# Down phase of a decoder step: second weight parts added by accumulating transfers, weight differences on VectorE, h loads given out earlier

## The chip, the cores and the metric

The kernel is one program on one core of a Trainium2 chip. It is judged by its time on the device in microseconds, the median of several runs. Five queues matter here: TensorE (PE), VectorE (DVE), ScalarE (ACT), GpSimd (POOL) and SyncE (SP). Each works its own instructions strictly in order and meets the others through semaphores only.

## What is computed

One step of a two-layer decoder: an mLSTM layer, then a layer of sliding-window attention, each followed by an MLP with squared ReLU, over 1024 prompt tokens and 32 sample tokens (1056 columns), width 1024, inner width 4096, all in float32.

```python
def sq_relu_mlp(x, w_up, w_down):
    h = jax.nn.relu(x @ w_up)
    return (h * h) @ w_down

# in trunk, after each layer's mixer
x = x + sq_relu_mlp(rmsnorm(x, norm_ffn[l]), w_up[l], w_down[l])
```

The change touches only the second product of each MLP, `(h * h) @ w_down`, which is done once in each layer.

## The kernel before

**Tiling.** Activations lie transposed: a feature per partition, 1056 tokens along the row. Every float32 operand is cut into a high and a low half (fp32r), and every product is three matmuls, high x high, low x high, high x low. ScalarE makes the high half (a copy), VectorE the low half (operand minus high half).

**The up phase** computes h in 16 blocks f = 0 to 15 of 256 inner features. Block f's rows z are scaled by VectorE (`scaled`) and stored to HBM as `h_rows` by SP (`store_h`), two rows of 528 KB a block. z lies in `z_even` for even f, in `act_a` and `act_b` for odd f.

**The down phase** takes blocks 0 to 13 by a scheme of seven products (Strassen's kind, table `DOWN`): w_down is quartered into parts (mh, kh) and h into parts (kh, nh); each product multiplies one part, or the sum or difference of two, of each. A product has KG = 7 groups, so q = 0 to 48 counts the groups; blocks 14 and 15 are left as a tail (q = 49 to 52) whose rows are computed plainly (`last_rows`, `last_down`). For a product i = q // 7:

| product | weight parts | h parts |
|---|---|---|
| 0 | (1,0) + (1,1) | (0,0) |
| 1 | (1,1) | (1,0) - (0,0) |
| 2 | (1,0) - (0,0) | (0,0) + (0,1) |
| 3 | (0,0) | (0,1) - (1,1) |
| 4 | (0,0) + (1,1) | (0,0) + (1,1) |
| 5 | (0,0) + (0,1) | (1,1) |
| 6 | (0,1) - (1,1) | (1,0) + (1,1) |

**A group q** goes like this. SP gives out `load_w(q)`: the first weight part into `down_raw(q)`, one of three buffers (`w_raw`, `w_raw_odd`, `w_third`, by q % 3), and, where the table has a second part, that one into `down_other(n)`, one of two buffers. Pool's `down_sum` (L1500) adds or subtracts the two in place (semaphore dw_sum). ScalarE's `w_high` (L1068) and VectorE's `w_low` (L1670) make w_hi and w_lo, two buffers each by q % 2. On the other side SP's `load_h` brings rows of h: parts (0,0), (0,1) and (1,1) once each, into b11, b12 and b22, which stay; part (1,0), in products 1 and 6, anew for each group into b21_even and b21_odd in turn. VectorE's `t_sum_of_h` (L1698) adds or subtracts two parts into t_sum_of, ScalarE (L1085) and VectorE (`t_low_of`, L1678) make t_hi and t_lo, in a ring of three. TensorE (`down`, L2762 to L2764) then does 48 matmuls of 264 columns. After each product ScalarE stages PSUM into act_a and act_b (`stage`, L1098), and VectorE adds that to x_res (`add_staged`, L1705) during the next product.

**The order.** It is written out by hand. `down_step(q)` on VectorE is w_low(q), t_low_of(q + 1), perhaps add_staged, t_sum_of_h(q + 2), perhaps h_low. On SP the loop is `load_h(q + 1)`, `load_w(q)`. The waits that matter: load_w(q) from q = 3 waits for w_low(q - 3); a load into b21 waits for the t_sum that read the same buffer two groups before; w_high(q) waits until TensorE is done with group q - 2. At the start of the phase SP has

```python
load_h(0)
load_h(1)
load_h(2)
load_w(1)
load_h(3)
load_w(2)
store_h(NF - 1)
```

The functions that the change touches, with the line numbers of the profile:

## Time and profile before

| what | us |
|---|---|
| median of three runs | 2336.6 (2334.8 to 2339.12) |
| the profiled execution's own time | 2334.56 |
| its span | 2332.7 |
| TensorE busy | 2251.5 (97%) |
| VectorE busy | 1566.6 (67%) |
| ScalarE busy | 1072.2 (46%) |
| Pool busy | 498.0 (21%) |
| down phase of layer 0 | about 898 to 1201 |
| down phase of layer 1 | about 1959 to 2262 |

TensorE is busy nearly all the time, so the kernel's time is TensorE's work plus the places where TensorE waits. In a timeline row the first number is the start, the second the time taken, and the bracket at the end is how long the engine had been idle before and what ended it. Rows of one kind that follow each other are merged, with their count.

### The profile page before, as it was taken

The numbers are of one execution on the slowest core, as the hardware profiler recorded it, in microseconds if no ns is written. First come the engines' busy times: TensorE is split into PE (matmuls) and PEld (weight loads), VectorE is DVE, ScalarE is ACT, GpSimd is POOL, SyncE is SP. The second block draws the span as 40 slices with busy tenths as digits, with TensorE's granted clock in tenths as the row PEclk, the third lists the DMA queues.
The fourth block names the chain that finished last, engine by engine and source line by source line (L and its number), as shares of the span: only waits on it lengthen the run. The fifth ranks groups of instructions, "written<-read, shape, count | busy, mean of one in ns | idle before, by whom it ended". The sixth has DMA issues, their size and how long they took to land. (4 is left out here: it accounts for less than half of the span.)

```text
span 2332.7 us, 41472 instructions
## 1 busy us (share of the span) xinstructions
PE 2251.5 (97%) x16886; PEld 2149.1 (92%) x16886; DVE 1566.6 (67%) x2516; ACT 1072.2 (46%) x2058; POOL 498.0 (21%) x403
## 2 busy tenths in 40 slices
PE   8999999999999999999989999999999999999989
PEld 7989898888999999999989877869999999999988
DVE  6555555569765566888966666565855666798873
ACT  4233222245766664433423454254666664343435
POOL 1000000013222223114312011013122223123323
PEclk9999999999999999999999999999999999999999
DMA  4111121102233336656631312101233336665541
GB/s 130 37 51 57 51 70 40 43 23 65 93 100 103 111 111 238 231 190 204 206 127 48 100 28 53 37 10 46 92 103 101 111 105 217 225 224 182 201 154 75
DMA packets 220928, 256.28 MB, mean 110 GB/s; under 512 B 27687, under 2 KB 144340, under 8 KB 220708
## 3 DMA queue, kind: packets, MB, share of 16 engines
q1 hardware_dynamic: 220596, 253.61, 33.4%
q8 instruction: 135, 2.21, 0.4%
q14 instruction: 53, 0.43, 0.1%
q10 hardware_dynamic: 144, 0.02, 0.0%
HBM read 211.84 MB, written 46.93 MB: 111 GB/s over the span
## 5 line engine op out<-in xcount | busy, mean ns | idle before, releaser
L2762 PE MATMUL acc<-t_hi,w_hi 128*128 128x264 f32 x1568 | 448.5, 286 | 23.0 <-DVE w_lo L1670 23.0
L2764 PE MATMUL acc<-t_hi,w_lo 128*128 128x264 f32 x1568 | 448.7, 286 | 0.0
L2763 PE MATMUL acc<-t_lo,w_hi 128*128 128x264 f32 x1568 | 448.7, 286 | 0.0
L2762 PEld LDWEIGHTS acc<-t_hi,w_hi 128*128 128x128 f32 x1568 | 297.8, 190 | 26.4 <-DVE w_lo L1670 26.4
L2764 PEld LDWEIGHTS acc<-t_hi,w_lo 128*128 128x128 f32 x1568 | 296.5, 189 | 0.0
L2763 PEld LDWEIGHTS acc<-t_lo,w_hi 128*128 128x128 f32 x1568 | 296.4, 189 | 0.0
L2728 PE MATMUL acc<-x_lo,w_hi 128*128 128x264 f32 x896 | 254.6, 284 | 0.0
L2729 PE MATMUL acc<-x_hi,w_lo 128*128 128x264 f32 x896 | 254.5, 284 | 0.0
L2727 PE MATMUL acc<-x_hi,w_hi 128*128 128x264 f32 x896 | 254.4, 284 | 0.0
L2483 PE MATMUL acc<-x_hi,w_hi 128*128 128x352 f32 x576 | 193.1, 335 | 1.4 <-DVE pair L1955 1.4
L2727 PE MATMUL acc<-T_hi,w_hi 128*128 128x264 f32 x672 | 190.9, 284 | 0.2
L2728 PE MATMUL acc<-T_lo,w_hi 128*128 128x264 f32 x672 | 190.7, 284 | 0.0
L2729 PE MATMUL acc<-T_hi,w_lo 128*128 128x264 f32 x672 | 190.3, 283 | 0.0
L2485 PE MATMUL acc<-x_hi,w_lo 128*128 128x352 f32 x576 | 185.8, 323 | 0.0
L2484 PE MATMUL acc<-x_lo,w_hi 128*128 128x352 f32 x576 | 185.4, 322 | 0.0
L2727 PEld LDWEIGHTS acc<-x_hi,w_hi 128*128 128x128 f32 x896 | 168.8, 188 | 0.0
L2728 PEld LDWEIGHTS acc<-x_lo,w_hi 128*128 128x128 f32 x896 | 168.7, 188 | 0.0
L2729 PEld LDWEIGHTS acc<-x_hi,w_lo 128*128 128x128 f32 x896 | 168.4, 188 | 0.0
L1678 DVE TENSOR_TENSOR t_lo<-t_sum_of,t_hi 128x1056 fp32r<-128x1056 f32 x70 | 132.3, 1890 | 1.8
L2727 PEld LDWEIGHTS acc<-T_hi,w_hi 128*128 128x128 f32 x672 | 126.6, 188 | 0.7 <-DVE w_lo L1643 0.7
L2728 PEld LDWEIGHTS acc<-T_lo,w_hi 128*128 128x128 f32 x672 | 126.6, 188 | 0.0
L2729 PEld LDWEIGHTS acc<-T_hi,w_lo 128*128 128x128 f32 x672 | 126.1, 188 | 0.0
(396 smaller groups left out, 5705.2 us busy)
## 6 DMA issues: line engine op xcount, KB each, us to landing
w_raw<-in_w_down SPq DMA_DIRECT2D x72, 512.0 KB, 5.0
w_raw_odd<-in_w_down SPq DMA_DIRECT2D x70, 512.0 KB, 4.9
b<-h_rows SPq DMA_DIRECT2D x42, 528.0 KB, 6.3
w_third<-in_w_down SPq DMA_DIRECT2D x34, 512.0 KB, 4.5
h_rows<-z_even SPq DMA_DIRECT2D x32, 528.0 KB, 2.7
w_raw<-in_w_up SPq DMA_DIRECT2D x32, 512.0 KB, 4.6
w_raw_odd<-in_w_up SPq DMA_DIRECT2D x32, 512.0 KB, 5.2
w_raw<-in_w_mlstm_in SPq DMA_DIRECT2D x24, 512.0 KB
```

Of the source, the lines that this page charges most:

```text
L1678: V.tensor_tensor(lo[:], src, hi[:].bitcast(F32), ALU.subtract).then_inc(dt_lo, 1)
L2483: T.matmul(block_of(g), hi, mh[:, span(b)], start=(kk == 0), stop=False)
L2484: T.matmul(block_of(g), hi, ml[:, span(b)], start=False, stop=False)
L2485: x = T.matmul(block_of(g), lo, mh[:, span(b)], start=False, stop=(kk == n_k - 1))
L2727: T.matmul(out[:, q], hi[:, k], mh[:, k, v], start=(k == 0), stop=False)
L2728: T.matmul(out[:, q], hi[:, k], ml[:, k, v], start=False, stop=False)
L2729: x = T.matmul(out[:, q], lo[:, k], mh[:, k, v], start=False, stop=(k == 3))
L2762: T.matmul(out[:, h], hi[:, c, rows], mh[:, c, v], start=(g == 0 and c == 0), stop=False)
L2763: T.matmul(out[:, h], hi[:, c, rows], ml[:, c, v], start=False, stop=False)
L2764: x = T.matmul(out[:, h], lo[:, c, rows], mh[:, c, v], start=False, stop=(g == KG - 1 and c == 1))
```

## The change

On SP, the order at the start of the down phase and the number of semaphores for the resident h loads are altered: all seven loads of product 0 are given out first, each waits for the landing of the one two before it (it was four), and the store of the last block's rows moves behind load_w(4). For products with a sum (0, 4, 5) SP no longer loads the second weight part. Pool issues a transfer from HBM that adds the second part onto the first in SBUF (`add_part`); it waits for the first part's landing and for the transfer two before it. For products with a difference (2, 6) SP loads both parts as before, and VectorE subtracts (`down_sum`), in step q for group q + 2, ahead of t_sum_of_h. ScalarE's w_high waits for whichever it is. At the end of the phase VectorE's w_low for the last three tail weights moves between the additions of the first rows.

```diff
-W_SUMS = [q for q in range(NG) if DOWN[q // KG][1] is not None]
+W_SUMS = [q for q in range(NG) if DOWN[q // KG][1] == SUB]
+W_ADDS = [q for q in range(NG) if DOWN[q // KG][1] == ADD]
...
-                    if op is not None:
+                    if op == SUB:
...
-                            if n >= 4:
-                                sp.wait_ge(db_loaded[n % 4], 16 * (turns(layer, n, len(RESIDENT), 4) - 1))
+                            if n >= 2:
+                                sp.wait_ge(db_loaded[n % 2], 16 * (turns(layer, n, len(RESIDENT), 2) - 1))
...
-                load_h(0)
-                load_h(1)
-                load_h(2)
+                for q in range(KG):
+                    load_h(q)
                 load_w(1)
-                load_h(3)
                 load_w(2)
-                store_h(NF - 1)
                 for q in range(3, NW):
-                    if q + 1 < NG:
+                    if KG <= q + 1 < NG:
                         load_h(q + 1)
                     load_w(q)
+                    if q == 4:
+                        store_h(NF - 1)
...
+                elif q in W_ADDS:
+                    n = W_ADDS.index(q)
+                    act.wait_ge(dw_added[n % 2], 16 * turns(layer, n, len(W_ADDS), 2))
...
-            def down_sum(layer, q):
-
-                n = W_SUMS.index(q)
+            def add_part(layer, q):
+
+                n, (mh, kh) = W_ADDS.index(q), DOWN[q // KG][2]
+                f = KG * kh + q % KG
+                part = io["w_down"][layer][2 * P * f:2 * P * f + 2 * P, 512 * mh:512 * mh + 512].rearrange("(k p) m -> p k m", p=P)
                 pool.wait_ge(dw_loaded[q % 3], 16 * turns(layer, q, NW, 3))
-                pool.wait_ge(dv_loaded[n % 2], 16 * turns(layer, n, len(W_SUMS), 2))
-                nc.gpsimd.tensor_tensor(down_raw(q), down_raw(q), down_other(n), DOWN[q // KG][1]).then_inc(dw_sum, 1)
+                if n >= 2:
+                    pool.wait_ge(dw_added[n % 2], 16 * (turns(layer, n, len(W_ADDS), 2) - 1))
+                pool.dma_start(down_raw(q).rearrange("p (k m) -> p k m", k=2), part, accum_op=ADD).then_inc(dw_added[n % 2], 16)
...
+            def down_sum(layer, q):
+
+                n = W_SUMS.index(q)
+                dve.wait_ge(dw_loaded[q % 3], 16 * turns(layer, q, NW, 3))
+                dve.wait_ge(dv_loaded[n % 2], 16 * turns(layer, n, len(W_SUMS), 2))
+                V.tensor_tensor(down_raw(q), down_raw(q), down_other(n), DOWN[q // KG][1]).then_inc(dw_sum, 1)
...
+                if q + 2 in W_SUMS:
+                    down_sum(layer, q + 2)
                 if q + 2 in T_SUMS:
                     t_sum_of_h(layer, q + 2)
...
+                    if n < 2 * TAIL - 1:
+                        down_step(0, NG + 1 + n)
...
                     last_row(0, k)
+                    if 0 < k < 2 * TAIL:
+                        down_step(1, NG + k)
...
-                for q in range(2, NW):
+                for q in range(2, NG + 1):
                     down_step(layer, q)
```

How the instructions stand, at the places that the prediction speaks of. First SP at the start of the down phase of layer 0, before the change, from the last block's neighbour to load_w(3) (b11 is the resident part (0,0) of h):

```order
L797 DMA h_rows0<-z_even 128x1056 [waits zz_ready] x2
L839 DMA b11<-h_rows0 128x2x528 [waits h_stored0,up_done]
L839 DMA b11<-h_rows0 128x2x528 [waits h_stored1,up_done]
L839 DMA b11<-h_rows0 128x2x528 [waits h_stored0,up_done]
L818 DMA w_raw_odd<-in_w_down 128x2x512 [waits op_lo]
L824 DMA w_raw_odd<-in_w_down 128x2x512
L839 DMA b11<-h_rows0 128x2x528 [waits h_stored1,up_done]
L818 DMA w_third<-in_w_down 128x2x512 [waits h_stored0]
L824 DMA w_raw<-in_w_down 128x2x512 [waits dw_sum]
L797 DMA h_rows0<-act_b 128x1056 [waits zz_ready]
L797 DMA h_rows0<-act_a 128x1056 [waits zz_ready]
L839 DMA b11<-h_rows0 128x2x528 [waits db_loaded0,h_stored0,up_done]
```

The same place with the change, from the third load of h on:

```order
L841 DMA b11<-h_rows0 128x2x528 [waits db_loaded0,h_stored0,up_done]
L841 DMA b11<-h_rows0 128x2x528 [waits db_loaded1,h_stored1,up_done]
L841 DMA b11<-h_rows0 128x2x528 [waits db_loaded0,h_stored0,up_done]
L841 DMA b11<-h_rows0 128x2x528 [waits db_loaded1,h_stored1,up_done]
L841 DMA b11<-h_rows0 128x2x528 [waits db_loaded0,h_stored0,up_done]
L820 DMA w_raw_odd<-in_w_down 128x2x512 [waits op_lo]
L820 DMA w_third<-in_w_down 128x2x512 [waits h_stored0]
L820 DMA w_raw<-in_w_down 128x2x512 [waits dw_lo]
L820 DMA w_raw_odd<-in_w_down 128x2x512 [waits dw_lo]
L799 DMA h_rows0<-act_b 128x1056 [waits zz_ready]
L799 DMA h_rows0<-act_a 128x1056 [waits zz_ready]
```

The four loads of h that stood behind load_w(1) are now ahead of it, five of them with a wait for an earlier one's landing, and the stores went behind load_w(4).

VectorE in product 6 of layer 0, steps 43 and 44, before:

```order
L1670 TENSOR_TENSOR w_lo<-w_raw_odd,w_hi 128x1024 [waits dw_hi]
L1678 TENSOR_TENSOR t_lo1<-t_sum_of,t_hi1 128x1056 [waits dt_hi]
L1705 TENSOR_TENSOR x_res<-x_res,act_a 128x2x528 [waits staged_rows]
L1698 TENSOR_TENSOR t_sum_of<-b21_even,b22 128x1056 [waits db_loaded1,ds_loaded0,dt_lo]
L1670 TENSOR_TENSOR w_lo<-w_third,w_hi 128x1024 [waits dw_hi]
L1678 TENSOR_TENSOR t_lo2<-t_sum_of,t_hi2 128x1056 [waits dt_hi]
L1705 TENSOR_TENSOR x_res<-x_res,act_b 128x2x528 [waits staged_rows]
L1698 TENSOR_TENSOR t_sum_of<-b21_odd,b22 128x1056 [waits db_loaded2,ds_loaded1,dt_lo]
```

The same steps with the change:

```order
L1684 TENSOR_TENSOR w_lo<-w_raw_odd,w_hi 128x1024 [waits dw_hi]
L1692 TENSOR_TENSOR t_lo1<-t_sum_of,t_hi1 128x1056 [waits dt_hi]
L1719 TENSOR_TENSOR x_res<-x_res,act_a 128x2x528 [waits staged_rows]
L1678 TENSOR_TENSOR w_raw<-w_raw 128x1024 [waits dv_loaded0,dw_loaded0]
L1712 TENSOR_TENSOR t_sum_of<-b21_even,b22 128x1056 [waits db_loaded1,ds_loaded0,dt_lo]
L1684 TENSOR_TENSOR w_lo<-w_third,w_hi 128x1024 [waits dw_hi]
L1692 TENSOR_TENSOR t_lo2<-t_sum_of,t_hi2 128x1056 [waits dt_hi]
L1719 TENSOR_TENSOR x_res<-x_res,act_b 128x2x528 [waits staged_rows]
L1678 TENSOR_TENSOR w_raw_odd<-w_raw_odd 128x1024 [waits dv_loaded1,dw_loaded1]
L1712 TENSOR_TENSOR t_sum_of<-b21_odd,b22 128x1056 [waits db_loaded2,ds_loaded1,dt_lo]
```

A difference with waits for two landings now stands ahead of each t_sum_of. And SP at the same place with the change, where only the line numbers differ from before; the dt_sum that a b21 load waits for is set by VectorE's t_sum_of:

```order
L850 DMA b21_odd<-h_rows0 128x2x528 [waits h_stored1,dt_sum]
L820 DMA w_raw_odd<-in_w_down 128x2x512 [waits dw_lo]
L826 DMA w_raw<-in_w_down 128x2x512 [waits dw_sum]
L850 DMA b21_even<-h_rows0 128x2x528 [waits h_stored0,dt_sum]
L820 DMA w_third<-in_w_down 128x2x512 [waits dw_lo]
L826 DMA w_raw_odd<-in_w_down 128x2x512 [waits dw_sum]
```

Nothing moved here: the h load still stands ahead of the two weight parts.

## Rows read from the trace of the kernel before

**Rows 1.** Waits: engine, line, releaser, us in total, times, longest.

```profile
PE acc L2762 <- DVE w_lo L1670: 23.0, 16, 3.8
```

**Rows 2.** Timeline of TensorE, its longer idle times in and behind both down phases.

```profile
904.50 0.39 PE L2762 MATMUL acc<-t_hi,w_hi 128*128 128x264 f32 x1 [0.67 <-DVE w_lo L1670]
920.30 0.39 PE L2762 MATMUL acc<-t_hi,w_hi 128*128 128x264 f32 x1 [3.80 <-DVE w_lo L1670]
...
1188.69 0.39 PE L2762 MATMUL acc<-t_hi,w_hi 128*128 128x264 f32 x1 [2.90 <-DVE w_lo L1670]
1209.49 0.43 PE L2785 MATMUL acc<-h_hi,w_hi 128*128 128x352 f32 x1 [3.04 <-DVE x_res L1732]
...
1980.71 0.59 PE L2762 MATMUL acc<-t_hi,w_hi 128*128 128x264 f32 x1 [3.61 <-DVE w_lo L1670]
...
2236.67 0.39 PE L2762 MATMUL acc<-t_hi,w_hi 128*128 128x264 f32 x1 [2.60 <-DVE w_lo L1670]
2250.36 0.39 PE L2762 MATMUL acc<-t_hi,w_hi 128*128 128x264 f32 x1 [1.69 <-DVE w_lo L1670]
2270.53 0.69 PE L2677 MATMUL acc<-h_hi,w_hi 128*128 128x384 f32 x1 [5.03 <-DVE x_res L1772]
```

**Rows 3.** Timeline of VectorE, two sums of h parts before product 6.

```profile
1144.98 1.25 DVE L1698 TENSOR_TENSOR t_sum_of<-b_odd,b 128x1056 f32<-128x1056 f32 x1
...
1156.70 1.26 DVE L1698 TENSOR_TENSOR t_sum_of<-b_odd,b 128x1056 f32<-128x1056 f32 x1
```

**Rows 4.** Timeline of SP's queue behind the second of them.

```profile
1157.98 0.37 SPq L848 DMA_DIRECT2D b_odd<-h_rows  x1
...
1158.91 0.47 SPq L824 DMA_DIRECT2D w_raw_odd<-in_w_down  x1
```

**Rows 5.** Timeline of Pool, its sums of weight parts in product 6.

```profile
1152.84 2.71 POOL L1500 TENSOR_TENSOR w_raw_odd<-w_raw_odd 128x1024 f32<-128x1024 f32 x1 [10.03 <-DMA w_raw_odd<-in_w_down]
1158.87 2.48 POOL L1500 TENSOR_TENSOR w_third<-w_third,w_raw 128x1024 f32<-128x1024 f32 x1 [3.32 <-DMA w_raw<-in_w_down]
1165.68 2.51 POOL L1500 TENSOR_TENSOR w_raw<-w_raw,w_raw_odd 128x1024 f32<-128x1024 f32 x1 [4.33 <-DMA w_raw_odd<-in_w_down]
```

**Rows 6.** Timeline of VectorE: one step of product 1, and one operation of product 6.

```profile
958.42 1.22 DVE L1670 TENSOR_TENSOR w_lo<-w_raw_odd,w_hi 128x1024 fp32r<-128x1024 f32 x1 [1.14 <-ACT w_hi L1068]
959.56 1.25 DVE L1678 TENSOR_TENSOR t_lo<-t_sum_of,t_hi 128x1056 fp32r<-128x1056 f32 x1
960.73 1.25 DVE L1705 TENSOR_TENSOR x_res<-x_res,act_a 128x1056 f32<-128x1056 f32 x1
961.90 1.25 DVE L1698 TENSOR_TENSOR t_sum_of<-b_odd,b 128x1056 f32<-128x1056 f32 x1
964.28 1.23 DVE L1670 TENSOR_TENSOR w_lo<-w_third,w_hi 128x1024 fp32r<-128x1024 f32 x1 [1.14 <-ACT w_hi L1068]
...
1159.17 3.29 DVE L1678 TENSOR_TENSOR t_lo<-t_sum_of,t_hi 128x1056 fp32r<-128x1056 f32 x1
```

**Rows 7.** Timeline of SP's queue at the start of the down phase, layer 0.

```profile
907.35 0.34 SPq L797 DMA_DIRECT2D h_rows<-act_a  x1
...
908.22 0.84 SPq L818 DMA_DIRECT2D w_raw<-in_w_down  x1
```

**Rows 8.** Timeline of ScalarE: its first read of b11 in layer 0.

```profile
890.19 1.09 ACT L1085 ACTIVATE t_hi<-b 128x1056 fp32r<-128x1056 f32 x1 [3.20 <-DMA b<-h_rows]
```

**Rows 9.** DMA issues: destination, queue, count, KB each, median us to landing.

```profile
w_raw<-in_w_down SPq DMA_DIRECT2D x72, 512.0 KB, 5.0
...
w_third<-in_w_down SPq DMA_DIRECT2D x34, 512.0 KB, 4.5
...
b_even<-h_rows SPq DMA_DIRECT2D x14, 528.0 KB, 4.0
```

**Rows 10.** Windows: stretch, busy us of PE, PEld, DVE, ACT, POOL, clock, DMA, GB/s.

```profile
920.30:926.20 5.90, 5.90 (x35) 5.90 (x36) 5.83 (x3) 2.03 (x2) 4.64 (x2) 0.71 1.05 392
...
1980.70:1986.60 5.90, 5.89 (x28) 5.89 (x29) 5.83 (x2) 2.03 (x2) 4.55 (x2) 0.53 1.05 392
...
2270.50:2276.00 5.50, 5.47 (x17) 5.47 (x18) 2.02 (x4) 0.00 (x0) 0.00 (x0) 0.50 0.00 0
```

More of the change, by code:

```diff
@@ L611, in build @@
         dv_loaded = [sem(f"dv_loaded{i}") for i in range(2)]
-        db_loaded = [sem(f"db_loaded{i}") for i in range(4)]
+        db_loaded = [sem(f"db_loaded{i}") for i in range(2)]
         ds_loaded = [sem(f"ds_loaded{i}") for i in range(2)]
         ht_loaded = sem("ht_loaded")
+        dw_added = [sem(f"dw_added{i}") for i in range(2)]
         dw_sum = sem("dw_sum")
@@ L836, in load_h @@
                             sp.wait_ge(h_stored[f % 2], 32 * ((NF // 2) * layer + f // 2 + 1))
-                            if n >= 4:
-                                sp.wait_ge(db_loaded[n % 4], 16 * (turns(layer, n, len(RESIDENT), 4) - 1))
+                            if n >= 2:
+                                sp.wait_ge(db_loaded[n % 2], 16 * (turns(layer, n, len(RESIDENT), 2) - 1))
                             sp.dma_start(down_h(q, half), h_rows[layer][2 * f:2 * f + 2, :, HALVES[nh]].rearrange("c p n -> p c n")
-                                         ).then_inc(db_loaded[n % 4], 16)
+                                         ).then_inc(db_loaded[n % 2], 16)
                     if q in STREAMED:
@@ L1082, in t_high_of @@
                     n = RESIDENT.index((half, g))
-                    act.wait_ge(db_loaded[n % 4], 16 * turns(layer, n, len(RESIDENT), 4))
+                    act.wait_ge(db_loaded[n % 2], 16 * turns(layer, n, len(RESIDENT), 2))
                     src = down_h(q, half)
@@ L1506, in mlp @@
                         weight_sum(layer, f, j)
-                for q in W_SUMS:
-                    down_sum(layer, q)
+                for q in W_ADDS:
+                    add_part(layer, q)
             nc.gpsimd.memset(eps_sum[:], DV * EPS).then_inc(ol_ready, 1)
@@ L1686, in h_landed @@
                     n = RESIDENT.index((half, q % KG))
-                    dve.wait_ge(db_loaded[n % 4], 16 * turns(layer, n, len(RESIDENT), 4))
+                    dve.wait_ge(db_loaded[n % 2], 16 * turns(layer, n, len(RESIDENT), 2))
             def t_sum_of_h(layer, q):
```

## The prediction

> **What bounds the kernel now.** I read the waits of TensorE first: in the down phases it sat idle 23.0 us before L2762, in 16 places, and every time the low half of the weights (w_lo, VectorE, L1670) came last [rows 1]. Next its timeline, for where. Group q=1 of layer 0 starts 0.67 us late and q=3 3.80 us late, q=3 of layer 1 3.61 us late; in product 6 there are 2.90 us in layer 0 and 2.60 and 1.69 in layer 1; behind the down phases come 3.04 and 5.03 us, with VectorE's additions to x_res as what ended them [rows 2]. So the start costs 8.08, product 6 costs 7.19, the other ten places of rows 1 cost 23.0 - 8.08 - 7.19 = 7.73, the two ends cost 8.07: 31.1 us in all. More than that, with what the slow clock behind a stall costs, this change can't win.
>
> Then VectorE, for how full it is. A group of TensorE takes 5.86 us (two w_lo rows, 958.42 and 964.28). In it lie w_lo, t_lo, an addition and t_sum, 1.14, 1.17 and 1.17 us from start to start, and 1.14 us is left over, idle until ScalarE's high half is there [rows 6]. The last row of that group is the other form of such an operation: t_lo at 1159.17 took 3.29 us, and Pool's sum began at 1158.87 and took 2.48 [rows 5, 6]. VectorE stood still while Pool ran. That is the source of most of the small stalls. The Trainium skill's page SBUF — State Buffer, section Who interferes with whom, has the rule: a VectorE operation with two SBUF inputs and a GpSimd one that reads SBUF exclude each other. The trace agrees: 3.29 against 1.25 us.
>
> **The change, part by part.** The sum is made against the profiled execution, 2334.56 us, which is 2.04 below the median of the runs, 2336.6.
>
> *Pool's sums go.* Of 70, 42 become transfers that Pool gives out and 28 go to VectorE; what stands behind them in Pool's queue (the sums of squares) starts later than they end. No operation of VectorE is held up by Pool any more in the down phases. The ten smaller places are of that kind: -7.7. (Products 0, 4 and 5 then have at most four operations of 1.17 a group on VectorE, 4.7 of 5.86 us, five in two groups of product 5.)
>
> *Product 2, differences on VectorE.* Five operations in four of the groups: 1.14 + 4 x 1.17 = 5.8 of 5.86 us. It fits, w_lo is ready some 3.5 us before it is wanted (5.86 less 1.06 of ScalarE and 1.2 of its own), and the loads for it don't wait for VectorE's sums. 0 us; if it didn't fit by 0.3 us, four groups use 1.2 of those 3.5.
>
> *Product 6, the same on VectorE: here a loop closes.* SP gives out, for group q+2, first the h load of q+3, which waits until t_sum(q+1) has read the other b21 buffer, and then w and its second part. Before, Pool waited for these. Now VectorE does, and t_sum(q+2) stands behind the difference in its queue, and lets the next loads go. One turn: from the end of a t_sum to Pool's start on the landed parts it is 6.61 us (1144.98 + 1.25 to 1152.84) or 7.72 (1156.70 + 1.26 to 1165.68) [rows 3, 5]; the SP rows between show the issues, 1157.98 and 1158.91 [rows 4]. The second came upon an earlier burst; with turns further apart I take 7.0. Plus 1.15 for the difference and 1.25 for the t_sum [rows 3, 6]: a turn is 9.4 us, against 5.86 for a group. Set time 0 at the end of group 39, where t_sum(42) ends (from the end of group 38: ScalarE 1.06, then four operations of 1.17). t_sum(43) ends at 9.4, t_sum(44) at 18.8, and w_lo(43) behind it at 20.0; group 43 could start at 3 x 5.86 = 17.6: 2.4 late. From there each group is a turn: 9.4 - 5.9 = 3.5 late, for 44, 45 and 46. Group 47 is free, since nothing holds the loads of 48. That is 2.4 + 3 x 3.5 = 12.9 a layer, 25.8 in two, where 7.2 stand now: +18.6. With 6.6 in place of 7.0 it is 10.9 a layer, with 7.7 16.4: -4 and +7.
>
> *The start.* Now the parts for q=3 are given out at 908.22, since SP waits to 907.35 for the last rows of h [rows 7]; that is where the 3.80 comes from. With store_h behind load_w(4) it goes. But all seven h loads now stand ahead of load_w(1), and each waits for the one two before it. h(0) landed by 890.19 [rows 8]. In pairs at 4.0 us, the time of such a load in the b21 buffers [rows 9], h(2) is there at 894.1, h(4) at 898.1, and h(6) and load_w(1) go out at about 898.5. Before, load_w(1) stood behind three of them and its second part right after it. It lands 5.0 later [rows 9], 903.5. Then comes the accumulating transfer, of which the trace has none. Bounds: a plain load of w_third's kind, 4.5 us, from below, and twice the plain 5.0 from above, 10.0. I take 7.0: it fetches as much from HBM, reads the SBUF side besides, and Pool issues it. 910.5, plus 1.06 and 1.2 for the halves: group 1 can start at 912.8. Group 0 is done at 904.50 - 0.67 = 903.8. That is 9.0 us of idle a layer, 18.0 in two, for 8.1: +9.9. With 4.5 or 10.0 for the transfer, -5 or +6; with 5.0 for the pairs, +4. Behind ScalarE's wait for this transfer (w_hi(1)) stand the ReLU and square of the last block's other half, then VectorE's scaling and SP's store of it: some 9 us later than now, but load_w(3) and load_w(4) no longer wait for the store, and the first stage of product 0 that needs act_a comes 41 us after group 0's start.
>
> The Trainium skill's page DMA: Bandwidth & Descriptors, section Anatomy of one DMA, gives a plain GpSimd transfer 2.0 us plus its bytes at 436 GB/s, 3.2 us for 512 KB; by that, if adding cost nothing, the start would be 5.2 us a layer and the whole 7.6 us less than I say. No row here shows one.
>
> Later in products 0, 4 and 5 the transfer is covered: w_lo(q-3) is done 2.3 us into group q-4, group q starts 21.1 us after that, and 5.0 + 7.0 + 2.3 = 14.3 are needed. That cover is gone at 13.8 us a transfer for a single one, and in the long run at 10.3 (three buffers, 17.6 us for three groups, less 7.3).
>
> *The ends.* In the last rows of layer 0 three w_lo and two additions stood between TensorE's first rows and VectorE's first addition of them; now one w_lo stands ahead and three come one by one between. TensorE had two rows done at 1209.49 - 3.04 = 1206.45 [rows 2]; the first is 2.9 us older, 1203.6, and VectorE, with 1.25 us, has taken it by 1204.9, before the third row wants its banks: -3.0. Layer 1: TensorE asks for the fourth row's bank at 2270.53 - 5.03 = 2265.5, and the first, ready some 2 us before, is taken by then; but three w_lo of 1.2 fall between additions that TensorE meets every microsecond, and I leave 0.8 for that: -4.2. Together -7.2.
>
> *The clock.* After 3.80 us of idle the granted clock was 0.71 over 5.9 us, after 3.61 us 0.53, and after 5.03 us 0.50 over 5.5 us [rows 10]: TensorE at the lower of its two levels, 1.2 GHz, for 3.4 to 5.9 us, so 1.7, 2.8 and 2.8 us lost. The last goes: -2.8. At the start both stay and may each be like the longer: +1.1. In product 6 the loop covers a slower group.
>
> Sum: -7.7 + 0 + 18.6 + 9.9 - 7.2 - 2.8 + 1.1 = **+11.9 us**; on the median 2336.6 that is **2348.5 us**.
>
> **The rivals.**
>
> *Faster: landings and adds at their short ends.* If a turn's wait is 6.2 and the transfer 4.5, with h pairs at 3.7: product 6 is 0.8 + 3 x 2.7 = 8.9 a layer (+10.6), the start 5.9 a layer (+3.7), so 10.6 + 3.7 + 0.5 - 17.7 = -2.9: 2333.7. For it: single loads land in 4.0 and 5.0 [rows 9]. Against: with three given out together neither of the two turns shown took under 6.6 [rows 3, 5]. The sign changes where 10 x (7.0 - wait) + 2 x (7.0 - transfer) passes 12.
>
> *Much slower: the transfer is the bound.* If it takes over 10.3 us, three buffers no longer keep 5.86 a group. At 15: (5.0 + 15 + 2.3) / 3 = 7.4, 1.6 a group over 42 groups, 67 less some 14 of lead, and 16 more at the start: 2336.6 + 11.9 + 69 = 2417. It decides from 10.3 on. For it: nothing in the trace shows such a transfer at all. Against: it would have to be three times a plain one of the same bytes [rows 9].
>
> *A port.* Pool must write the transfer's descriptors while VectorE has two inputs in SBUF almost all the time. If that shuts them out as Pool's sums were (3.29 for 1.25), each transfer is longer by one or two operations of VectorE, 1.2 to 2.4 us, and two more at the start per layer: 2351 to 2353, and small stalls stay. The Trainium skill's page SBUF — State Buffer, same section, speaks both ways: VectorE's two-port modes lock out the writing of descriptors, and such a sum of two tensors takes only the read side; the latter is marked as inferred there.
>
> **How the numbers follow.** The forecast's case 0.55 (2343 to 2362), the short ends 0.25 (2328 to 2343, half of it under 2331.9), the transfer as bound 0.12 (over 2372), the port 0.08. The sign hangs on the loop in product 6, which follows from the order of instructions, and on the unknown transfer. The range, 2330 to 2372, leaves out the slow transfer and the last part of the short ends. A measurement of this kernel can tell about 0.2%, 4.7 us: faster by more 0.13, within 0.19, slower by more 0.68.
>
> **What would show it.** In product 6 VectorE's differences each wait for a transfer, every 9 to 10 us, and TensorE idles about 3.5 us before three groups of each layer; no Pool sums, and no 3.3 us operations on VectorE. At the start one idle time of 7 to 11 us before group 1 and none before group 3. At the ends under 1 us. I am wrong if product 6 runs at 5.9 a group (then it is -7 or so), or if TensorE waits in products 4 and 5.

## The result

| | before | after |
|---|---|---|
| median of four runs, us | 2336.6 (2334.8 to 2339.1) | 2384.8 (2383.9 to 2385.9) |
| the profiled execution's own time, us | 2334.56 | 2383.96 |
| its span, us | 2332.7 | 2382.2 |
| mean granted clock of TensorE | 0.992 | 0.985 |
| PE busy, us | 2251.5 | 2264.9 |
| VectorE busy, us | 1566.6 | 1470.8 |
| Pool busy, us | 498.0 | 357.4 |

The ratio is 1.0193 (95%: 1.0174 to 1.0212): 48 us slower. The forecast was 2348.5, from 2330 to 2372. The direction was right, the size was not: 11.9 us were forecast, four times as much came.

The waits of TensorE in the profile after (engine, line, releaser, us in all, times, longest), to be read beside [rows 1]:

```profile
PE acc L2782 <- DVE w_lo L1684: 64.1, 36, 11.8
...
PE acc L2782 <- ACT act_a L1102: 1.9, 2, 1.0
```

The waits for low halves have gone from 23.0 to 64.1 us, from 16 places to 36. The timeline of TensorE tells where; these are the first group of each kind, to be read beside [rows 2]:

```profile
918.00 0.59 PE L2782 MATMUL acc<-t_hi,w_hi 128*128 128x264 f32 x1 [11.78 <-DVE w_lo L1684]
...
1148.72 0.39 PE L2782 MATMUL acc<-t_hi,w_hi 128*128 128x264 f32 x1 [0.66 <-DVE w_lo L1684]
1155.44 0.39 PE L2782 MATMUL acc<-t_hi,w_hi 128*128 128x264 f32 x1 [0.58 <-DVE w_lo L1684]
...
1194.62 0.39 PE L2782 MATMUL acc<-t_hi,w_hi 128*128 128x264 f32 x1 [2.91 <-DVE w_lo L1684]
1203.75 0.59 PE L2782 MATMUL acc<-t_hi,w_hi 128*128 128x264 f32 x1 [3.00 <-DVE w_lo L1684]
1212.83 0.39 PE L2782 MATMUL acc<-t_hi,w_hi 128*128 128x264 f32 x1 [1.60 <-DVE w_lo L1684]
...
2000.36 0.59 PE L2782 MATMUL acc<-t_hi,w_hi 128*128 128x264 f32 x1 [10.25 <-DVE w_lo L1684]
```

There are three kinds. The **start** is one idle time of 11.78 us in layer 0 and one of 10.25 in layer 1. **Product 6** is five idle times a layer or four, 11.9 us in layer 0 and 11.6 in layer 1. New, and not forecast, are the 25 others, most of them 0.5 to 0.8 us long (three are 1.3 to 1.9), before most groups of products 0, 4 and 5: in the two rows of product 5 above the groups stand 6.72 us apart, where TensorE takes 5.86. Behind the down phases nothing is left of the 3.04 and 5.03 us of [rows 2].

Why one group takes 6.7 us there is in the timeline of Pool, whose only work at that time is to give out the accumulating transfers (the second number is the time of giving out; the bracket tells how long Pool had waited):

```profile
909.10 1.24 POOL L1507 DMA_DIRECT2D w_raw_odd<-in_w_down  x1 [26.61 <-DMA w_raw_odd<-in_w_down]
915.82 1.21 POOL L1507 DMA_DIRECT2D w_third<-in_w_down  x1 [5.48 <-DMA w_raw_odd<-in_w_down]
922.62 1.22 POOL L1507 DMA_DIRECT2D w_raw<-in_w_down  x1 [5.60 <-DMA w_third<-in_w_down]
930.39 1.20 POOL L1507 DMA_DIRECT2D w_raw_odd<-in_w_down  x1 [6.55 <-DMA w_raw<-in_w_down]
937.27 1.21 POOL L1507 DMA_DIRECT2D w_third<-in_w_down  x1 [5.68 <-DMA w_raw_odd<-in_w_down]
```

Each begins when the one before has landed: the transfer of 915.82 is into w_third, and what ended Pool's wait was the landing in w_raw_odd, of the transfer of 909.10. The program doesn't ask for that. `add_part` waits for its own first part, which SP gave out at 901.92, and for the transfer two before, which was over. So the transfers run one at a time. The issues of the profile (destination, queue, count, KB, median us to landing) say how long one takes:

```profile
w_third<-in_w_down SPq DMA_DIRECT2D x34, 512.0 KB, 4.8
...
w_raw<-in_w_down POOLq DMA_DIRECT2D x14, 512.0 KB, 6.5
w_raw_odd<-in_w_down POOLq DMA_DIRECT2D x14, 512.0 KB, 6.5
```

6.5 us each (the prediction took 7.0), and so one in about 6.75 us. The transfer's length was forecast well; that two would be under way at once was not so.

Product 6, SP's queue. The h load waits for VectorE's t_sum, and the two weight parts stand behind it:

```profile
1175.45 0.37 SPq L850 DMA_DIRECT2D b_even<-h_rows  x1
1175.86 0.47 SPq L820 DMA_DIRECT2D w_third<-in_w_down  x1
1176.37 0.47 SPq L826 DMA_DIRECT2D w_raw_odd<-in_w_down  x1
1184.42 0.37 SPq L850 DMA_DIRECT2D b_odd<-h_rows  x1
1184.83 0.47 SPq L820 DMA_DIRECT2D w_raw<-in_w_down  x1
```

And VectorE at the same time, where L1678 is the difference and L1712 the t_sum behind it:

```profile
1181.99 1.22 DVE L1678 TENSOR_TENSOR w_third<-w_third,w_raw_odd 128x1024 f32<-128x1024 f32 x1 [3.10 <-DMA w_raw_odd<-in_w_down]
1183.14 1.25 DVE L1712 TENSOR_TENSOR t_sum_of<-b_odd,b 128x1056 f32<-128x1056 f32 x1
...
1191.03 1.23 DVE L1678 TENSOR_TENSOR w_raw<-w_raw 128x1024 f32<-128x1024 f32 x1 [3.01 <-DMA w_raw<-in_w_down]
1192.17 1.25 DVE L1712 TENSOR_TENSOR t_sum_of<-b_even,b 128x1056 f32<-128x1056 f32 x1
```

Here the loop of the prediction is seen turning: t_sum ends at 1184.39, the h load goes out at 1184.42, the weights behind it, their landing ends VectorE's wait at 1191.03, the next t_sum ends at 1193.42, the next h load goes out at 1193.45. A turn is 9.03 us; 9.4 were forecast.

Where the 49.4 us between the two profiled executions went, by these rows: the start 22.0 for 8.1 (+13.9); product 6 23.5 for 7.2 (+16.3); the other waits for w_lo 18.6 for 7.7 (+10.9); the waits for act_a, which only show once TensorE has fallen behind, +1.9; the ends 0.2 for 8.1 (-7.9). That is 35.1. A stop also costs a little beside its own length: of the 6.72 us above, 5.86 are work and 0.58 idle, 0.28 are left. At about 0.25 for each of 20 more places that is 5, an estimate. The rest is the clock. Windows of 2 us over the whole run, each with its PE busy time times the missing part of the granted clock, sum to 7.3 us in the down phases before and 14.5 after (+7.2), and to 1.7 and 5.1 in a stretch of the first up phase where both programs are alike (+3.4); elsewhere it is 2.1 less. Together 48.6 of 49.4. Each clock sum is that of one execution, and the granted clock differs between executions of one kernel: in the four of the kernel with the differences alone on VectorE (below) the mean went from 0.983 to 0.987 and the time from 2364.1 to 2353.6 us. So the idle times here are shown, and the clock's share only to within some us.

### The profile page after: what moved, and what is told of

Its sections match the earlier page's. It is cut to its first block and busy times, and to the rows that moved or that the text cites. A ratio compares the mean times of both kernels' runs of the same rounds, so it can differ in the third digit from the quotient of the medians.

```text
span 2382.2 us, 41426 instructions
## 1 busy us (share of the span) xinstructions
PE 2264.9 (95%) x16886; PEld 2157.5 (91%) x16886; DVE 1470.8 (62%) x2544; ACT 1068.5 (45%) x2058; POOL 357.4 (15%) x375
## 5 line engine op out<-in xcount | busy, mean ns | idle before, releaser
L2782 PE MATMUL acc<-t_hi,w_hi 128*128 128x264 f32 x1568 | 455.6, 291 | 66.2 <-DVE w_lo L1684 64.1
L1057 ACT ACTIVATE w_hi<-s_tmp 128x512 fp32r<-128x512 f32 x84 | 52.7, 627 | 157.8 <-POOL s_tmp L1493 93.9
```

The costliest lines, as they stand in the source:

```text
L1057: nc.scalar.activation(w_slot(w_hi, up_slot(f, j), 4), up_source(f, j), ACT.Copy).then_inc(op_hi, 1)
L2782: T.matmul(out[:, h], hi[:, c, rows], mh[:, c, v], start=(g == 0 and c == 0), stop=False)
```

## The experiments

Each is given as its ratio to the kernel before, run beside it on the same chip. Medians of the kernel before differed from set to set (2337.0, 2341.3 and 2340.2 us), so differences between sets are made from the ratios, on 2336.6. The row of the transfers in halves rests on two executions only.

| kernel | median, us | ratio (95%) | TensorE's waits for w_lo, us |
|---|---|---|---|
| after | 2384.8 | 1.0193 (1.0174 to 1.0212) | 64.1 in 36 |
| after, more room for descriptors | 2359.1 | 1.0090 (1.0071 to 1.0109) | 47.2 in 14 |
| after, weights ahead of h in product 6 | 2351.6 | 1.0060 (1.0043 to 1.0077) | 41.4 in 31 |
| after, old order at the start | 2372.4 | 1.0144 (1.0127 to 1.0161) | 53.5 in 38 |
| after, transfers in halves | 2360.2 | 1.0087 (1.0067 to 1.0107) | 46.5 in 14 |
| before, ends alone | 2327.0 | 0.9957 (0.9942 to 0.9971) | 22.8 in 16 |
| before, store_h alone | 2327.3 | 0.9951 (0.9938 to 0.9964) | 16.4 in 14 |
| before, differences on VectorE alone | 2358.9 | 1.0083 (1.0056 to 1.0109) | 34.1 in 15 |
| after, all three mended | 2307.8 | 0.9859 (0.9843 to 0.9876) | 12.0 in 7 |
| before, three moves, sums on Pool | 2314.5 | 0.9894 (0.9878 to 0.9911) | 14.5 in 18 |
| the same, differences on VectorE | 2303.7 | 0.9840 (0.9824 to 0.9857) | 5.4 in 5 |

### The room for descriptors

```diff
-    nc = _bacc.Bacc(..., dynamic_dma_scratch_size=1024)
+    nc = _bacc.Bacc(..., dynamic_dma_scratch_size=2048)
```

> The changed kernel with 2048 instead of 1024 bytes of each partition kept for the descriptors that Pool writes; nothing else differs. In the changed kernel Pool begins each accumulating transfer only when the one before it has landed (909.10, 915.82, 922.62, 930.39), one in about 6.75 us against 5.87 us per group of TensorE. Theory A (the room for descriptors holds one transfer): now two are in flight, Pool's issues come in pairs closer than 6.5 us, the 0.5 to 0.9 us of idle before each group of products 0, 4 and 5 go, some 15 groups a layer at 0.9: 2384.8 - 27 = 2358, between 2350 and 2366. Theory B (the queue or the DMA engines do one at a time whatever the room): no change, 2384.8 within 2. Theory C (two at once share a limit and each takes 13 us): no change either, but the issues come in pairs and a transfer takes twice as long.

It gave 25.7 us back by the medians (24 by the ratios). Pool's timeline:

```profile
906.25 1.21 POOL L1507 DMA_DIRECT2D w_raw_odd<-in_w_down  x1 [26.17 <-DMA w_raw_odd<-in_w_down]
907.52 1.20 POOL L1507 DMA_DIRECT2D w_third<-in_w_down  x1
...
1124.29 1.20 POOL L1507 DMA_DIRECT2D w_third<-in_w_down  x1 [9.49 <-DMA w_third<-in_w_down]
1125.48 1.25 POOL L1507 DMA_DIRECT2D w_raw<-in_w_down  x1
```

The second issue follows the first after 1.2 us, with no wait. In TensorE's timeline two idle times of 1.00 and 0.83 us are left in products 0, 4 and 5, of the 18.6 us; of the 47.2 us that stay, 22.1 are the start and 23.3 product 6. Theory A holds, B falls. There is something of C in it: the median to landing of the transfers into w_raw_odd and w_third rose to 9.0 and 8.2 us. Two under way slow each other, but by these medians the pair takes some 9.5 us from the first issue, where one after the other took 13.5.

### The same transfers in halves

```diff
-                pool.dma_start(down_raw(q).rearrange(...), part, accum_op=ADD).then_inc(dw_added[n % 2], 16)
+                for k in range(2):
+                    pool.dma_start(down_raw(q)[:, 512 * k:512 * k + 512], part[:, k], accum_op=ADD).then_inc(dw_added[n % 2], 16)
...
```

The waits for dw_added, on Pool and on ScalarE, count 32 for a group instead of 16.

> The changed kernel with each accumulating transfer given out as two of half the size (256 KB), still 1024 bytes for descriptors. Theory A (the room for descriptors is what lets only one be under way, and it is counted by the transfer's size): two halves fit, the second issue follows the first by about 1.2 us, and a group takes no longer than before, 2365 to 2390. Theory B (one transfer at a time, whatever its size): each half costs a fixed time of its own, some 4 to 5 us, so 8 to 10 a group in place of 6.75, 36 groups and more of 2 us: 2440 or more.

```profile
911.65 1.77 POOL L1508 DMA_DIRECT2D w_raw_odd<-in_w_down  x2 [26.61 <-DMA w_raw_odd<-in_w_down]
912.94 1.37 POOL L1508 DMA_DIRECT2D w_third<-in_w_down  x1
917.48 0.86 POOL L1508 DMA_DIRECT2D w_third<-in_w_down  x1 [3.16 <-DMA w_raw_odd<-in_w_down]
```

Three halves go out back to back. The fourth is the second half of the same weights as the third, with no wait of its own in the program, and still it stands 3.16 us, until w_raw_odd has landed. So it isn't the number of transfers that is limited but what they need together. The list of queues has the packets and MB of Pool's queue, first with whole transfers, then with halves:

```profile
q0 software_dynamic: 11424, 22.02, 6.0%
```
```profile
q0 software_dynamic: 12096, 22.03, 5.7%
```

The 42 whole ones have 272 packets each, the 84 halves 144. With 1024 bytes three halves (432 packets) are let through and neither a fourth (576) nor two whole ones (544). Counted by size it would be 768 KB let through and 1024 KB not; which of the two is counted these runs don't tell. At 2360.2 us it did better than theory A's range (2365 to 2390), and as well as the doubled room, since in the rows above up to three halves overlap.

### Weights ahead of h in product 6

```diff
-                    if KG <= q + 1 < NG:
+                    last = q >= (NPROD - 1) * KG
+                    if KG <= q + 1 < NG and not last:
                         load_h(q + 1)
                     load_w(q)
+                    if q + 1 < NG and last:
+                        load_h(q + 1)
```

> The changed kernel with the loads of product 6 in another order on SP: the weights of group q ahead of the h load of q+1, so that the difference of group q no longer waits behind t_sum(q-1) and the h load. Theory A (the loop through t_sum, SP and the landing, one turn per group): a turn now covers two groups, 9.4 us against 11.7, product 6 falls from 52.2 and 55.3 us to some 41 to 44, so 2384.8 - 22 = 2363, between 2358 and 2368. Theory B (VectorE is full in product 6, five operations of 1.15 us in 5.87): the idle time falls by half at most, 2373 or more. Products 0, 4 and 5 as they were.

By the medians 33.2 us came back (31 by the ratios), more than the 22 of theory A, and 2351.6 lies below its range. SP's queue in product 6:

```profile
1174.30 0.37 SPq L850 DMA_DIRECT2D b_odd<-h_rows  x1
1175.44 0.37 SPq L820 DMA_DIRECT2D w_raw_odd<-in_w_down  x1
1175.85 0.47 SPq L826 DMA_DIRECT2D w_raw_odd<-in_w_down  x1
1180.25 0.37 SPq L850 DMA_DIRECT2D b_even<-h_rows  x1
```

The h loads now stand 5.95 us apart, and TensorE has no idle time over 0.35 us in product 6 of either layer. 23.5 us were idle there in the kernel after; most of the rest is the clock, whose mean rose from 0.985 to 0.991 (summed as above, from the first down phase to the end, without layer 1 ahead of its down phase, 5.1 us are lost to it, for 14.5). So VectorE, with five operations in 5.9 us, is full but fast enough; theory B falls.

### The differences alone on VectorE

In the kernel before, `down_sum` of products 2 and 6 moves from Pool to VectorE's step, with a semaphore of its own; the resident h loads give one up and have three.

```diff
+                if q + 2 in W_SUMS and DOWN[(q + 2) // KG][1] == SUB:
+                    down_sum(layer, q + 2)
                 if q + 2 in T_SUMS:
                     t_sum_of_h(layer, q + 2)
```

> The kernel before with the differences of products 2 and 6 on VectorE and nothing else: no accumulating transfers, the loads, the start and the ends in their old order. Theory A (the loop in product 6 comes from the differences standing ahead of t_sum on VectorE with the old order of the loads, whatever the sums of products 0, 4 and 5 are done by): product 6 has some 12.5 us of idle a layer where 3.6 stand, with the slow clock 20 in all: 2358, between 2351 and 2364. Theory B (product 6 was late in the changed kernel because the accumulating transfers had used up the lead): at most 5 us slower than before, 2342 or less.

It came out at 2358.9, where 2358 was expected (between 2353.6 and 2364.1 in four executions). Two of its idle times in product 6:

```profile
1175.14 0.48 PE L2778 MATMUL acc<-t_hi,w_hi 128*128 128x264 f32 x1 [2.84 <-DVE w_lo L1684]
...
1193.43 0.59 PE L2778 MATMUL acc<-t_hi,w_hi 128*128 128x264 f32 x1 [3.09 <-DVE w_lo L1684]
```

In both layers together product 6 has 20.4 us of them, for 7.2 before. Some 12.5 a layer were expected and 10.7 and 9.8 came, so that the time hit so closely is in part luck: the slow clock took more than was allowed for it. The loop doesn't need the accumulating transfers; it comes from this one step.

### The old order at the start

```diff
-                for q in range(KG):
-                    load_h(q)
+                load_h(0)
+                load_h(1)
+                load_h(2)
                 load_w(1)
+                load_h(3)
                 load_w(2)
                 for q in range(3, NW):
-                    if KG <= q + 1 < NG:
+                    if q + 1 < NG:
```

> The changed kernel with SP's order at the start of a down phase as in the kernel before (three h loads ahead of load_w(1), the fourth ahead of load_w(2), the others one by one), and store_h still behind load_w(4). Theory A (load_w(1) behind seven h loads makes the start): load_w(1) goes out some 13 us earlier, the accumulating transfer of 6.5 us has landed before group 0 ends, the 11.8 and 10.3 us of idle before group 1 fall to under 1, and since the transfers are then ahead of TensorE by some 5 us, the small stalls of product 0 go too; with what the slow clock cost, 2384.8 - 26 = 2359, between 2352 and 2364. Theory B (something else holds group 1, such as ScalarE's high half behind the last block of the up phase): the idle before group 1 stays above 5 us, 2372 or more.

A miss: 2372.4, 12.4 us off where 26 were expected, with 4.97 and 4.04 us still idle before group 1, and with the small stalls of product 0, which were to go as well, still there. SP, Pool and ScalarE tell why:

```profile
884.08 7.59 SPq L841 DMA_DIRECT2D b<-h_rows  x3
891.72 0.46 SPq L820 DMA_DIRECT2D w_raw_odd<-in_w_down  x1
```
```profile
897.04 1.24 POOL L1509 DMA_DIRECT2D w_raw_odd<-in_w_down  x1 [16.31 <-DMA w_raw_odd<-in_w_down]
```
```profile
907.07 1.06 ACT L1074 ACTIVATE w_hi<-w_raw_odd 128x1024 fp32r<-128x1024 f32 x1 [6.18 <-DMA w_raw_odd<-in_w_down]
```

Two things were left out of that expectation. The third h load waits for the landing of the first, since there are two semaphores for them where the kernel before has four, so load_w(1) goes out at 891.72. And the accumulating transfer, given out at 897.04, had landed only at 907.07, 10.0 us. That is most likely since SP's next loads now run beside it (a weight load given out at 896.89, an h load at 898.54), where the 6.5 us at the same place of the changed kernel had none beside them. With a sum on Pool there was 1 us of work in that place; with a transfer there are 6.5 to 10.

### The ends alone, and store_h alone

The first moves the tail's w_low between the last additions in the kernel before, the second store_h(NF - 1) behind load_w(4).

```diff
-                for q in range(2, NW):
+                for q in range(2, NG + 1):
                     down_step(layer, q)
...
+                    if n < 2 * TAIL - 1:
+                        down_step(0, NG + 1 + n)
...
+                    if 0 < k < 2 * TAIL:
+                        down_step(1, NG + k)
```

> The kernel before with one part of the change alone: VectorE's low halves of the tail groups between the additions of the last rows instead of ahead of them. Theory A (the prediction): the 3.04 and 5.03 us of idle behind the down phases fall by 3.0 and 4.2, and the slow clock behind the second goes, 2.8: 2336.6 - 10 = 2326.6, between 2325 and 2330. Theory B (the additions between which they stand then come late): 2332 or more.

```diff
                 load_w(2)
-                store_h(NF - 1)
                 for q in range(3, NW):
...
+                    if q == 4:
+                        store_h(NF - 1)
```

> The kernel before with one move alone: store_h of the last block behind load_w(4) in place of ahead of load_w(3). Theory A: the 3.80 and 3.61 us before group 3 go, and with them most of the 4.5 us that the slow clock cost behind them: 2336.6 - 10 = 2327, between 2324 and 2331. Theory B (the loads for group 3 are then late for another reason, such as the h loads): half of it or less, 2332 or more.

2327.0 and 2327.3 us, where 2326.6 and 2327 were expected (by the ratios 10.0 and 11.4 us). No idle time over 0.35 us is left behind either down phase in the first, none before group 3 in the second. These were the two good parts of the change, and they hold without the rest.

### Three kernels that beat both

The first is the changed kernel with 2048 bytes for descriptors, the order of the loads in product 6 as above, and at the start load_w(1) ahead of the third h load, with the h loads from the fifth on one by one in SP's loop:

```diff
-                for q in range(KG):
-                    load_h(q)
+                load_h(0)
+                load_h(1)
                 load_w(1)
+                load_h(2)
+                load_h(3)
                 load_w(2)
```

The other two are the kernel before with the diffs of the ends, of store_h and of the loads in product 6 (there without the bound KG on q + 1), the last of them with that of the differences too.

> The changed kernel with everything mended that the first runs point to: 2048 bytes for the descriptors, in product 6 the weights ahead of the h loads, at the start load_w(1) ahead of the third h load and the other h loads one by one. The first three runs took off 25.7, 33.2 and 12.4 us; the start should give 8 more, since its idle was still 5.0 and 4.0 us: theory A (the three causes are separate), 2384.8 - 79 = 2306, between 2300 and 2314. Theory B (they overlap: what one gives back, the next wait takes): 2320 or more. Against the two kernels whose sums stay on Pool it tells what adding by transfers is worth: nothing, if it is within 3 us of them.

> The kernel before with three moves of order and no other change, all sums still on Pool: store_h of the last block behind load_w(4) in place of ahead of load_w(3); in product 6 the weights of q ahead of the h load of q+1; the tail's low halves between the last additions. From 2327.0 of the last move alone: the 3.4 to 3.8 us before group 3 and what the slow clock cost there go (9 to 11), product 6 loses its 7.2 or most of it (5): theory A, 2312, between 2307 and 2318. Theory B (Pool's sums, which stand behind VectorE's two-input operations, hold product 6 whatever the order of the loads): its stalls stay, 2317 or more.

> The same three moves, and the differences of products 2 and 6 on VectorE, the sums of products 0, 4 and 5 on Pool. Against the run with all sums on Pool this prices the move of the differences by itself. Theory A (with the loop of loads opened, VectorE has room: five operations in 5.87 us): no stall in products 2 and 6, 1 to 4 us faster than with the sums on Pool. Theory B (VectorE is full): stalls of 0.3 to 1 us a group in product 6, 2 to 8 us slower.

The changed kernel with its three faults mended came to 2307.8 us, theory A: the causes are separate, they add up (by the ratios 78 us, where the three single experiments had given 67, the last of them with a less good order at the start). The kernel before with three moves of order alone came to 2314.5, in the range too. With the differences of products 2 and 6 on VectorE besides, it is the fastest, 2303.7, ratio 0.984; it ran in the same set as the one with the sums on Pool and is 10.8 us below it, not the 1 to 4 that were expected. The reason stands in VectorE's timeline of product 6. First with the sums on Pool:

```profile
1162.81 3.29 DVE L1682 TENSOR_TENSOR t_lo<-t_sum_of,t_hi 128x1056 fp32r<-128x1056 f32 x1
...
1168.36 1.21 DVE L1674 TENSOR_TENSOR w_lo<-w_raw,w_hi 128x1024 fp32r<-128x1024 f32 x1
1169.65 3.30 DVE L1682 TENSOR_TENSOR t_lo<-t_sum_of,t_hi 128x1056 fp32r<-128x1056 f32 x1
...
1175.22 1.21 DVE L1674 TENSOR_TENSOR w_lo<-w_raw_odd,w_hi 128x1024 fp32r<-128x1024 f32 x1
```

Pool's sum beside it:

```profile
1168.76 3.08 POOL L1504 TENSOR_TENSOR w_third<-w_third,w_raw_odd 128x1024 f32<-128x1024 f32 x1 [3.77 <-DMA w_raw_odd<-in_w_down]
```

And the same steps with the differences on VectorE:

```profile
1164.74 1.22 DVE L1688 TENSOR_TENSOR w_lo<-w_raw,w_hi 128x1024 fp32r<-128x1024 f32 x1
1166.03 1.26 DVE L1696 TENSOR_TENSOR t_lo<-t_sum_of,t_hi 128x1056 fp32r<-128x1056 f32 x1
1167.21 1.25 DVE L1723 TENSOR_TENSOR x_res<-x_res,act_a 128x1056 f32<-128x1056 f32 x1
1168.38 1.22 DVE L1682 TENSOR_TENSOR w_third<-w_third,w_raw_odd 128x1024 f32<-128x1024 f32 x1
1169.51 1.25 DVE L1716 TENSOR_TENSOR t_sum_of<-b_even,b 128x1056 f32<-128x1056 f32 x1
1170.68 1.22 DVE L1688 TENSOR_TENSOR w_lo<-w_raw_odd,w_hi 128x1024 fp32r<-128x1024 f32 x1
```

With Pool, one of VectorE's four operations a step takes 3.3 us and a step 6.86 (1168.36 to 1175.22): TensorE waits 0.6 to 0.9 us before four groups of product 6 in layer 0 and five in layer 1. Without Pool five operations take 5.94, and TensorE waits for nothing. VectorE has more to do and is done sooner. A Pool sum costs VectorE 2.0 us, doing it itself costs it 1.15. The Trainium skill's page SBUF — State Buffer, section Who interferes with whom, on which the prediction drew, says that a VectorE operation with two SBUF inputs contends with a Pool one that reads SBUF. The trace agrees: t_lo of 1169.65 ends 1.1 us after the Pool sum beside it.

What adding by transfers is worth can be read from the fastest against the mended one: 0.9840 against 0.9859, 4 us in favour of the sums on Pool, with intervals that overlap. The two also differ in the order at the start and in the semaphores of the h loads, so it isn't the price of that one part alone. In products 4 and 5 TensorE waits 4.1 us for w_lo with the transfers and 4.4 with the sums on Pool, so they buy nothing there. In product 0 it waits 2.77 us in layer 0 and 1.80 and 3.35 in layer 1 with the transfers, against 0.62 and 0.38.

## Why the prediction was too small

**The step that failed** is "Later in products 0, 4 and 5 the transfer is covered", with the cover gone "in the long run at 10.3". It counts three buffers and takes for granted that transfers overlap as far as the program allows. With one at a time (6.5 us each, one in about 6.75), cover is a matter of rate: it is gone as soon as a transfer takes longer than a group, 6.75 against 5.86 us. The rival "the transfer is the bound" was this mechanism with its threshold in the wrong place: it was said to decide from 10.3 us on, and it decided from 5.9. That moves the small places from the -7.7 forecast to +10.9, 18.6 us, and the doubled room took 24 to 26 away again. No row of before could show it, since Pool gives out no transfer there; how many can be under way should have been a bound of the sum, and wasn't. Between the profiled executions the sum is 37.5 us short (49.4 for 11.9). 18.6 are this term, 8.9 the clock in the down phases, 4.0 the start, about 5 (the estimate above) what a stop costs beside its length, and 1.9 the waits for act_a; product 6 and the ends came 3.0 lower than forecast: together 35.4.

**Product 6** was right in mechanism: the turn was forecast at 9.4 us and measured 9.03. That the total came so near, forecast 12.9 us a layer, measured 11.9 and 11.6, is in part luck. Groups 43 to 46, the ones forecast, waited only 9.2 and 8.4 us, and a stop before group 42, 2.73 and 3.12 us, was not forecast; its cause stays open. The two experiments with the order of the loads and with the differences alone bear it out.

**The start** was right in mechanism, short by 2.0 us a layer on average (9.0 forecast, 11.78 and 10.25). Step by step in layer 0: load_w(1) went out at 901.41 (898.5 forecast), the seven h loads taking 15.5 us:

```profile
885.84 15.52 SPq L841 DMA_DIRECT2D b<-h_rows  x7
901.41 0.46 SPq L820 DMA_DIRECT2D w_raw_odd<-in_w_down  x1
```

It landed after 7.7 us and not 5.0, with two more weight loads given out within 1 us of it; the transfer took 6.5 for 7.0. That is 2.9 + 2.7 - 0.5 = 5.1 later, less the 2.4 by which group 0 itself ended later than forecast.

**The clock** was forecast at -2.8 + 1.1 and measured at +7.2 in the down phases. What was left out is that the idle times of product 6 bring slow stretches of their own, and the longer start a longer one. A window of the start after (columns as in [rows 10]):

```profile
909.00:922.00 13.00, 4.00 (x18) 4.00 (x19) 3.65 (x3) 4.09 (x4) 2.45 (x2) 0.53 0.62 111
```

TensorE is idle for nine of these 13 us, and the clock is at 1.2 GHz in nearly all of it, the four busy ones too. In the kernel with the differences alone on VectorE, whose new stops are nearly all in product 6, the same sum is 23.8 us for 7.3. Of these 16.5 more, 10.5 stand in and right behind product 6, which has 13.2 us more idle time; 3.3 stand behind stops of 2.34 us in product 4, and 1.6 behind that of 3.04 us after the down phase of layer 0, where before has stops of 1.87, 2.33 and 3.04 us and no slow clock; 1.6 stand in the last 10 us of the run. In the kernel after it is 7.4 in product 6, for 16.3 more idle. So the clock takes about half to four fifths of the stalls' own time there, and a stop of the same length brings a slow stretch in one execution and none in another; what decides it stays open.

**The ends** (-7.2 forecast, -7.9 measured), **product 2** (0, and no wait over 0.35 us in it) and the **removal of Pool's sums** as a source of VectorE's 3.3 us operations were right. The **port** rival is excluded: giving out a whole transfer took Pool 1.20 to 1.25 us in every row above, in the kernel after 1.21 at 1991.40, where VectorE was idle, and 1.20 at 1073.35, where it was busy nearly throughout; and the doubled room, which changes nothing there, took the small waits away. This agrees with what the Trainium skill's page SBUF — State Buffer, section Who interferes with whom, marks as inferred: a tensor_tensor of VectorE takes only the read side of what it shares with Pool, and writing descriptors needs the write side.

## What to carry to other kernels

Before work is moved to a queue, ask for its rate, not only its latency: how many of its transfers can be under way, and what holds the next one back (here room for descriptors, set in one line of the program, which shows as an issue that begins only when the last one has landed). When an operation is moved onto an in-order engine, draw the loop that it closes, from the loads that it waits for to the load that its successor lets go; here one swap of two loads opened it again. And take a change apart: here two parts of five were worth 10 and 11 us by themselves, the differences on VectorE were worth 11 only with a swap beside them, and adding by transfers was worth nothing that could be measured, even with room for two.

## What the runs showed of the hardware

- An accumulating transfer of 512 KB from HBM to SBUF takes 6.5 us in the median with one at a time under way, 6.4 at the least and 10.9 at the most in the kernel after; a plain one of the same bytes from SP 4.5 to 5.6 in the medians. By the fit of the Trainium skill's page DMA: Bandwidth & Descriptors, section Anatomy of one DMA, a plain one from Pool would take 3.2, an estimate that no run here tests; the accumulating one takes twice that.
- Giving it out costs Pool 1.2 us, half the size mostly 0.86 to 0.89.
- With 1024 bytes of each partition for descriptors, one such transfer or three of 256 KB are under way; with 2048, two of 512 KB, 8.2 and 9.0 us each in the medians (the program allows no more than two).
- A sum of two tensors on Pool (128 x 1024) takes 2.5 to 3.1 us in the rows shown and stretches one operation of VectorE from 1.25 to 3.3 us.
